# One decoder step on one core: row statistics, weight low halves, key pages and the first head pair are scheduled otherwise

## The chip, the cores and the metric

The kernel runs on one core of a Trainium2 chip. Its time is the device time of one launch in microseconds (us); the number that counts is the median over the runs. The core has five engines with a queue each, which work side by side and meet at semaphores: PE (TensorE, matrix products), DVE (VectorE), ACT (ScalarE), POOL (GpSimd) and SP, which here only issues DMAs. PE is the engine with most to do, so an idle microsecond on PE is, nearly always, a microsecond of the run. Each queue is served strictly in order: an instruction that waits holds up all that stands behind it on its engine, and this is what most of the text below is about.

## The reference, cut to what matters

One layer of a hybrid decoder trunk, for a prompt (1024 positions) and 8 samples with one new token each, 1024 columns wide, all in fp32.

```
h = rmsnorm(x);  z = h @ w_in                      # 2308 columns, in blocks of 512, 260, 512, 512, 512
A: softmax(q k^T / 8 + forget bias), causal        # prompt; samples read 32 pages of 128 old keys each
B: u * (W_s v + b), inside chunks of 128 positions
C: dilated window attention, three branches, joint softmax; samples read windows of old keys
M: softmax(q mem_k^T / 8) into 256 memory rows     # mem_k, mem_v = rmsnorm(mem) @ w_mem
x = x + concat(norm(A), norm(B), norm(C), norm(M)) @ w_out
x = x + down(silu(conv(gate)) * conv(value))       # ConvFFN, 2 x 2816 columns up
```

`rmsnorm` divides a row by the root of the mean of its squares; here the products run on the unnormalised rows and the factor of each row is applied to the result. For a sample, attention A needs the dot products of its query with 4096 paged keys, then the weighted sum of 4096 paged values.

## The kernel before, in words

Each fp32 operand is split into a high half that PE takes (`hhi`, `whi`) and a low half, the rest (`hlo`, `wlo`); a product is three matmuls, hi*hi, hi*lo, lo*hi (L847 to L849).

**Start.** 16 chunks of the transposed input (`x_load`, `x_hi` on ACT at L1138, `x_lo` on DVE at L1475) and 8 chunks of the first weight block (`w_load`, `split_hi` on ACT at L1127, `split_lo` on DVE at L1466) come in through SP's queue. Then the same rows are fetched a second time, in row layout (`stat_load`, L467, 11 fetches, three places to put them), and ACT squares and sums each (L1159). POOL turns all 11 sums at once into row factors (`inverse_rms`, L2091 and L2094), and only then does ACT begin to evacuate the first product (`rs_row`).

**Projection.** There are 47 units (`units`): 5 blocks of columns (b) times the 8 samples ("S") and 8 tiles of 128 prompt rows, and two units of memory rows (b = 5). A unit is 8 chunks times 3 matmuls into one of 4 banks. Behind a unit ACT evacuates or squares it, DVE sums the squares (L1510), POOL makes the factor, DVE applies it one turn later (`finish_norm`, L1522 and L1530); SP writes the result out two turns later. The loops of all engines over the units are written out by hand, and what else stands in a turn is in this order. `chunk_turns` says in which turn a chunk of the next weight block is split: chunks 0 to 3 in units 0 to 3 of the block before, chunks 4 and 5 in its last unit, chunks 6 and 7 in the "S" unit of the block itself. One granule of sample keys (4 pages, 512 KB, in a ring of 4) stands in each of 32 prompt turns of blocks 1 to 4, at the turn's end (`k_dot`, L1498 and L1501). Two pages of a granule are issued by SP, two by ACT, each after reading its page number (L353, L354). Block 2 has the small products of group B behind its units (`sgu`, L822), each with a DVE gate (L1557) before the next.

**Attention.** When the last unit is done and all outputs have landed, the first head pair is loaded (`qk_load(0)`, `toe_load`), transposed (`prep`, L894) and split. Then come 96 steps: 4 heads of A (steps 0 to 31), 4 of M (32 to 63), 4 of C (64 to 95), 8 query tiles each. In a step PE does scores, transposes and the product with the values, DVE the maximum (`score`), ACT the exponential. Steps 0 to 31 also carry the other 32 key granules, whose 4 pages SP issues three steps ahead; after the 32nd and 64th granule DVE takes the maxima, POOL reduces them over the partitions (`max_all`, L2114), DVE subtracts. 74 granules of sample values are added by PE (`v_sum`, L962) from step 4 on, by the table `v_step`; POOL issues all four pages of the first `V1` = 22, later POOL two and SP two.

**Rest.** Output projection and ConvFFN follow.

## Time and profile before

| what | us |
|---|---|
| median of 3 runs (range) | 1607.78 (1606.0 to 1610.24) |
| the profiled execution, its own time | 1605.6 |
| its span, first to last instruction | 1604.0 |
| start, until the sixth unit begins | 0 to 62.2 |
| projection, from there to the last unit's end | 62.2 to 317.8 |
| change-over to attention, until step 4 | 317.8 to 365.1 |
| steps 4 to 15, steps 16 to 31 | 54.1, 75.5 |
| steps 32 to 63 (heads of M) | 97.9 |
| steps 64 to 95 (heads of C) | 592.6 to 698.5 |
| output projection and ConvFFN | 698.5 to 1604.0 |

PE is busy for 91% of the span, DVE 60%, ACT 29%, POOL 10%. The last 905 us are nearly pure PE work and the change leaves them alone. A step is counted from the moment at which DVE writes its maximum. The profile's chain that ended last gives PE 66% of the span, SP's queue 9%, DVE 9%, waiting for nothing visible 7%.

### The profile page before, as it was taken

What the parts mean: (1) busy time and instruction counts of PE and PEld (TensorE: products, weight loads), DVE (VectorE), ACT (ScalarE), POOL (GpSimd) and SP (SyncE); (2) the same over time, 40 slices, a digit from 0 to 9 for tenths busy, and PEclk for the clock granted to TensorE, in tenths of its full rate; (3) what the DMA queues carried; (4) which work ended last, traced back from release to release, by engine and by line L of the source; (5) the groups of instructions that cost most, each with busy time, mean ns of one, the idle gap of its engine ahead of it and who ended that gap; (6) DMA issues with size and microseconds to landing.
All of it is one profiled execution on the core that took longest, in us unless ns stands there. A gap on an engine that the chain in (4) does not pass through costs nothing.

```text
span 1604.0 us, 25881 instructions
## 1 busy us (share of the span) xinstructions
PE 1464.0 (91%) x8727; PEld 1318.3 (82%) x8727; DVE 955.9 (60%) x1528; ACT 466.2 (29%) x723; POOL 163.3 (10%) x262
## 2 busy tenths in 40 slices
PE   6897989858889999778989999999999999999997
PEld 4686777646666667568989999999999999999997
DVE  5365467659987766482466655565646556555553
ACT  5322112233433456451232322222212222222210
POOL 0300022223322233200000000000000000000000
PEclk9998999956855579888999999999999999999999
DMA  7484335387667957322100220202102020120202
GB/s 262 154 252 141 115 115 174 115 242 207 203 200 231 299 176 219 110 85 109 59 27 12 68 67 14 73 8 80 54 27 67 14 81 27 53 67 14 79 1 116
DMA packets 123224, 177.11 MB, mean 110 GB/s; under 512 B 23005, under 2 KB 94198, under 8 KB 122674
## 3 DMA queue, kind: packets, MB, share of 16 engines
q1 hardware_dynamic: 105290, 140.17, 28.0%
q0 software_dynamic: 9728, 27.80, 5.8%
q10 hardware_dynamic: 8064, 7.34, 1.6%
q8 instruction: 78, 1.28, 0.3%
...
## 4 chain that ended last, share of the span: by engine, by line
PE 66%; SPq 9%; DVE 9%; issue 7%; DMA 4%; ACT 3%; POOL 1%; POOLq 0%; ACTq 0%; DVEq 0%; PEldq 0%
PE ps L1017 16%; PE ps L1018 16%; PE ps L1019 16%; SPq L353 4%; SPq L354 4%; PE ps L943 3%; PE ps L847 3%; PE ps L849 2%; PE ps L848 2%; PE ps L962 2%; PE ps L927 1%; DMA qb<-in_x_prompt 1%; PE ps L918 1%; DMA vring<-in_cache_a_v 1%; DVE ring L1498 1%
## 5 line engine op out<-in xcount | busy, mean ns | idle before, releaser
L1017 PE MATMUL ps<-hhi,uhi 128*128 128x344 f32 x1056 | 339.0, 321 | 11.9 <-DVE hlo L1964 4.9
L1018 PE MATMUL ps<-hlo,uhi 128*128 128x344 f32 x1056 | 337.8, 320 | 0.0
L1019 PE MATMUL ps<-hhi,ulo 128*128 128x344 f32 x1056 | 337.5, 320 | 0.0
L1017 PEld LDWEIGHTS ps<-hhi,uhi 128*128 128x128 f32 x1056 | 199.3, 189 | 13.7 <-issue 10.6
L1018 PEld LDWEIGHTS ps<-hlo,uhi 128*128 128x128 f32 x1056 | 199.3, 189 | 0.0
L1019 PEld LDWEIGHTS ps<-hhi,ulo 128*128 128x128 f32 x1056 | 199.3, 189 | 0.0
L1017 PE MATMUL ps<-ahi,dhi 128*128 128x344 f32 x528 | 170.4, 323 | 3.6 <-DVE dlo L2067 3.6
L1018 PE MATMUL ps<-alo,dhi 128*128 128x344 f32 x528 | 170.5, 323 | 0.0
L1019 PE MATMUL ps<-ahi,dlo 128*128 128x344 f32 x528 | 169.6, 321 | 0.0
L847 PE MATMUL ps<-whi,hhi 128*128 128x512 f32 (+1 forms) x376 | 147.3, 392 | 20.8 <-DVE wlo L1466 12.7
L943 PEld LDWEIGHTS ps<-vst,pts 128*128 128x128 f32 x704 | 110.6, 237 | 62.2 <-issue 41.8
L1996 DVE TENSOR_TENSOR uu<-ps,rstd_bc 128x1032 f32<-128x1032 f32 x44 | 54.3, 1233 | 178.8 <-PE ps L1019 178.8
L849 PE MATMUL ps<-whi,hlo 128*128 128x512 f32 (+1 forms) x376 | 143.9, 383 | 0.0
L848 PE MATMUL ps<-wlo,hhi 128*128 128x512 f32 (+1 forms) x376 | 143.7, 382 | 0.0
L943 PE MATMUL ps<-vst,pts 128*128 128x65 f32 x704 | 124.4, 329 | 14.0 <-DVE oN L1691 13.8
L354 POOL DMA_DIRECT2D vring<-in_cache_a_v x172 | 93.1, 541 | 184.3 <-issue 175.6
L2029 DVE TENSOR_TENSOR x<-ps,x 128x1032 f32<-128x1032 f32 x80 | 98.3, 1229 | 14.6 <-PE ps L1019 11.0
L847 PEld LDWEIGHTS ps<-whi,hhi 128*128 128x128 f32 x376 | 73.7, 196 | 39.6 <-DVE wlo L1466 16.0
L1017 PEld LDWEIGHTS ps<-ahi,dhi 128*128 128x128 f32 x528 | 100.1, 190 | 5.5 <-DVE dlo L2067 3.9
L1019 PEld LDWEIGHTS ps<-ahi,dlo 128*128 128x128 f32 x528 | 100.2, 190 | 0.0
L1018 PEld LDWEIGHTS ps<-alo,dhi 128*128 128x128 f32 x528 | 100.2, 190 | 0.0
L1370 ACT ACTIVATE convG<-uu,prm_a 128x1024 f32<-128x1024 f32 x22 | 27.4, 1247 | 202.0 <-DVE uu L1996 202.0
...
## 6 DMA issues: line engine op xcount, KB each, us to landing
...
```

What stands on the lines that cost most here:

```text
L353: page = sp.value_load(ptab[0:1, bass.ds(seq * PAGES + (group * 4 + j), 1)], min_val=0, max_val=NPOOL - 1)
L354: sp.dma_start(dst[:, slot, j, :], pool[bass.ds(page, 1)].rearrange("o p c -> p (o c)"))\
L847: pe.matmul(out, lh, whi[:, sl, 0:w], start=(kc == 0), stop=False)
L848: pe.matmul(out, lh, wlo[:, sl, 0:w], start=False, stop=False)
L849: i = pe.matmul(out, ll, whi[:, sl, 0:w], start=False, stop=(kc == KC - 1))
L943: i = pe.matmul(ps[:, 6, 0:HD + 1], pts[:, g % 2, j, :], vst[:, hp % 2, j, H % 2, :], start=(j == 0), stop=(j == nb - 1))
L962: m = pe.matmul(ps[32 * q:32 * q + NH, 7, 0:WG], e_, v, start=first, stop=final)
L1017: pe.matmul(out, lhs_hi(kc), rhs_hi(kc)[:, cs], start=(n == 0), stop=False)
L1018: pe.matmul(out, lhs_hi(kc), rhs_lo(kc)[:, cs], start=False, stop=False)
L1019: i = pe.matmul(out, lhs_lo(kc), rhs_hi(kc)[:, cs], start=False, stop=(n == nk - 1))
L1996: dve.tensor_tensor(c3(uu[:, :]), U3(k % 2), c3(rstd_bc[:, :]), ALU.mult).then_inc(S("f_free"), 1)
L2029: dve.tensor_tensor(c3(x2[:, d, :]), U3(d % 2), c3(x2[:, d, :]), ALU.add).then_inc(S("f_free"), 1)
```

## The change

1. **Statistics.** The second fetch of the 9 input row tiles is gone. ACT squares each staged chunk (`x_square`, 16 of 516 columns), POOL adds them (`x_add`, 14 adds), PE sums over the partitions with 9 products with a column of ones (`stats`), DVE copies the sums in two parts (`stat_copy`), POOL makes the factors in three parts, so the first four units wait for the first half alone. The two tiles of memory rows are still fetched, later (`mem_stats`). The constants' DMAs move from SP to ACT's queue. The sums over forget-gate pages move from behind the "S" unit to behind unit (0, 2).
2. **Low halves of weights.** After the first block `split_lo` runs on POOL, in POOL's turn. `chunk_turns` puts chunks 4 to 7 all in the last unit of the block before, and the loads run 4 chunks ahead of the splits.
3. **Key pages.** 48 granules, not 32, are spread over the turns from (0, 6) to (5, 1) (`K_AT`, by a table of room per block), the first of a turn at its start; steps 0 to 15 carry the other 16. The softmax preparation of the first half moves into block 4 (`early_softmax` at (4, 3), `subtract_a(0)` at (4, 6), `max_all` on POOL at (4, 5)), that of the second half from steps 32 and 35 to 16 and 19.
4. **Values.** `V0, V1, V2 = 8, 28, 44`: 8 granules by step 15 (all four pages on POOL), 20 in steps 16 to 31, 16 in steps 32 to 63, 30 after; from the 9th on SP issues two of four pages.
5. **First pair.** Its queries and keys are loaded at turn (2, 2) into places of their own, its transposes use banks 4 and 5 and stand right behind the last unit; SP loads rows, values and bias table ahead of the last output.

The core of the diff:

```diff
-                        turns[u if kc < 6 else UI[(b, "S")] if b < 5 else UI[(5, 0)]].append((b, kc))
+                    turns[UI[(b - 1, kc if kc < 4 else 7)]].append((b, kc))
...
+        NKP = 48
+        for u_, (b_, t_) in enumerate(units):
+            if u_ >= UI[(0, 6)]:
+                k_room[u_] = (2.9, 2.2, 4.1, 2.9, 3.6, 2.0)[b_]
...
-        V1, V2 = 22, 46
+        V0, V1, V2 = 8, 28, 44
...
-            for x in range(11):
-                stat_load(x)
...
+                if k == (2, 2):
...
+                    qk_load(0)
...
-            qk_load(0)
+            sp.wait_ge(S("z_done"), NU)
             sp.wait_ge(S("crow_dram"), 64)
             c_rows(0)
-            outputs(units[NU - 1])
-            for s4 in range(4):
-                uses = [k for k in prompt_no if prompt_no[k] % 4 == s4]
-                sp.wait_ge(S(f"zo_out{s4}"), 16 * sum(0 if k[0] == 2 else n_out[k[0]] for k in uses))
+            v_load(0)
             sp.wait_ge(S("toe_dram"), 80)
...
             toe_load(toeA[:, :], 0, "toeA_ld")
-            v_load(0)
             for n in range(NKP, NKP + 3):
                 k_load(n)
...
-                if g < 32:
+                if g < 16:
                     k_load(NKP + 3 + g)
...
+            def stats(half):
+
+                pe.wait_ge(S("x_acc"), 8 * half + 8)
...
+                for x, c0 in cols:
+                    m = pe.matmul(ps[:, 7, 288 + x:289 + x], sacx[:, c0:c0 + P], ones[:, 0:1], start=True, stop=True)
+                m.then_inc(S("st_pe"), 1)
...
                 if k == (0, "S"):
+                    pe.wait_ge(S("rtab"), 4)
+                    stats(0)
+                    page_transposes()
+                if k == (0, 2):
+                    page_sums()
+                    pe.wait_ge(S("st_cp"), 1)
+                    stats(1)
...
+            def x_square(i):
+
+                c = slice((i // 8) * 516, (i // 8) * 516 + 516)
+                if i % 8 == 0:
+                    act.activation(sacx[:, c], xslot(i)[:, 0:516], ACT.Square).then_inc(S("x_sq"), 1)
+                else:
...
+                    act.activation((sqt0 if i % 2 else sqt1)[:, :], xslot(i)[:, 0:516], ACT.Square).then_inc(S("x_sq"), 1)
...
+                act.wait_ge(S("rs_row"), 1 if u < 4 else 2 if b < 5 else 3)
...
-                for bb, kc in CT[u]:
-                    split_lo(bb * KC + kc)
...
+                if grans:
+                    granule(grans.pop(0))
...
+                if k == (4, 3):
+                    early_softmax()
+                if k == (4, 6):
+                    subtract_a(0)
...
+            for u, k in enumerate(units):
+                for bb, kc in CT[u]:
+                    split_lo(bb * KC + kc)
...
+                if k == (4, 5):
+                    max_all(1, 0, 0, 16)
...
-                if k == 25:
+                if k == 17:
                     max_all(2, 0, 16, 32)
```

Three places show how it moves instructions. First DVE in the middle of block 3, where a turn joins the granule (`ring`), the sum of squares (`ssn`), the application of the factor (`zn`, `zo`) and the split (`wlo`). Before:

```order
L1498 TENSOR_TENSOR ring<-ring,qb 128x1024 [waits ring_ld1,qb_ld]
L1501 TENSOR_REDUCE sA<-ring 128x16 [waits k_mul]
L1466 TENSOR_TENSOR wlo<-wst,whi 128x512 [waits w_hi]
L1510 TENSOR_REDUCE ssn<-sq 128x8 [waits rs_norm,act_z]
L1522 SCALAR_TENSOR_TENSOR zn<-ps,rsx,rsn 128x512 [waits zo_dve,rs_norm]
L1530 TENSOR_TENSOR zo<-zn,prm_b 128x256 [waits dve_z,zo_out1,ob_ready]
```

and now:

```order
L1546 TENSOR_TENSOR ring<-ring,qb 128x1024 [waits ring_ld0,qb_ld]
L1549 TENSOR_REDUCE sA<-ring 128x16 [waits k_mul]
L1570 SCALAR_TENSOR_TENSOR zn<-ps,rsx,rsn 128x512 [waits zo_dve,rs_norm]
L1578 TENSOR_TENSOR zo<-zn,prm_b 128x256 [waits dve_z,zo_out2,ob_ready]
L1558 TENSOR_REDUCE ssn<-sq 128x8 [waits rs_norm,act_z]
```

The split with its wait for ACT (`w_hi`) has left DVE, and the wait for the unit itself (`act_z`) now stands behind the granule and the factor.

Second POOL at units (4, 5) to (4, 7), where `ISA small<-small` is the reduction over the partitions and a bare `ISA` exchanges the library that POOL's program is taken from. Before, the first reduction stands behind the last of the first 16 value pages (page number read, DMA), after the projection:

```order
L353 TENSOR_LOAD ptab
L353 ISA x2
L354 ISA
L354 DMA vring<-in_cache_a_v 128x256
L2114 ISA
L2114 ISA small<-small 128x16 [waits pm]
```

and now between normalisations of the projection:

```order
L2147 TENSOR_TENSOR rsn<-rsn,nhalf 128x4 [waits pool_chain]
L2150 ISA
L2150 ISA small<-small 128x16 [waits pm]
L2144 ISA
L2144 TENSOR_SCALAR rsn<-ssn 128x4 [waits zo_dve,ss_dve]
L2147 TENSOR_TENSOR rsn<-rsn,nhalf 128x4 [waits pool_chain]
L2165 TENSOR_TENSOR wlo<-wst,whi 128x512 [waits w_hi] x4
```

Two exchanges and the reduction stand ahead of the factor of unit (4, 6) and of the last four splits, which unit (5, 0) needs.

Third SP behind the last unit. Before:

```order
L572 DMA qst<-scr_q 128x8x128 [waits zo_out2,zo_out1,zo_out3,zo_out0,z_done]
L573 DMA kst<-o_ka 128x8x128
L591 DMA klc<-scr_c 2x1024 [waits crow_dram]
L516 DMA o_mk<-zo 128x256 [waits act_z,zo_dve]
L516 DMA o_mv<-zo 128x256
L587 DMA toeA<-scr_t 128x1024 [waits toe_dram,zo_dve,zo_out3,ob_out0,zo_out2,ob_out1,zo_out1,zo_out0]
```

and now:

```order
L582 DMA klc<-scr_c 2x1024 [waits crow_dram,z_done]
L573 DMA vst<-o_va 128x8x64 x2
L578 DMA toeA<-scr_t 128x1024 [waits zo_out0,toe_dram]
L356 TENSOR_LOAD ptab [waits k_used]
L356 ISA x2
L357 ISA
L357 DMA ring<-in_cache_a_k 128x256
```

The last output and the wait for it no longer stand between the last unit and the bias table and the key pages.

## Rows read from the trace of the kernel before

**Rows 1.** Stretches: start:end, us, busy us (x count) by engine, granted clock, DMA share, GB/s

```profile
62.20:69.96 7.76, 7.75 (x24) 6.17 (x25) 5.41 (x12) 0.03 (x1) 4.93 (x5) 0.70 0.57 174
62.20:317.80 255.60, 231.73 (x1077) 190.13 (x1077) 154.98 (x249) 54.44 (x102) 41.67 (x51) 0.94 0.51 155
87.08:118.56 31.48, 28.24 (x217) 27.59 (x217) 22.95 (x34) 7.66 (x16) 1.83 (x2) 0.95 0.90 270
118.56:131.44 12.88, 8.23 (x25) 5.73 (x25) 8.18 (x13) 6.06 (x10) 0.00 (x0) 0.74 0.95 313
143.13:163.10 19.97, 15.88 (x66) 12.97 (x65) 7.33 (x12) 3.59 (x7) 0.00 (x0) 0.83 0.20 60
189.50:222.90 33.40, 26.96 (x114) 21.74 (x114) 13.63 (x29) 4.99 (x8) 6.36 (x6) 0.90 0.23 68
264.10:297.40 33.30, 33.30 (x145) 27.01 (x144) 23.46 (x36) 10.15 (x23) 6.02 (x10) 1.00 0.55 170
317.80:365.10 47.30, 22.93 (x104) 18.98 (x105) 25.66 (x51) 15.65 (x22) 12.88 (x23) 0.63 0.79 225
365.10:419.20 54.10, 47.14 (x293) 35.27 (x292) 49.77 (x97) 21.99 (x39) 19.37 (x36) 0.72 0.69 204
419.20:494.70 75.50, 64.87 (x391) 49.42 (x390) 64.57 (x126) 26.18 (x45) 20.44 (x38) 0.70 0.65 191
494.70:592.60 97.90, 93.16 (x499) 60.70 (x500) 66.35 (x160) 43.52 (x124) 28.22 (x53) 0.59 0.82 252
592.60:633.20 40.60, 39.71 (x361) 29.82 (x359) 30.23 (x87) 26.16 (x50) 16.55 (x30) 1.00 0.84 250
698.50:1604.00 905.50, 869.61 (x5442) 862.59 (x5441) 499.35 (x596) 210.89 (x215) 3.84 (x6) 0.98 0.16 51
```

**Rows 2.** Chain of waits in the start: start us, us, what

```profile
29.24 4.90 DMA qb<-in_x_prompt
...
46.07 5.23 DMA qb<-in_mem
```

**Rows 3.** Instructions in order of time at the first evacuation: start us, us

```profile
52.56 0.23 POOL L2091 TENSOR_SCALAR rsx<-ssx 128x11 f32<-128x11 f32 x1 [41.33 <-ACT biasA L1159]
...
62.21 0.77 PE L847 MATMUL ps<-whi,hhi 128*128 128x512 f32 x1 [6.76 <-issue]
```

**Rows 4.** Who waited in 62 to 318: total us, times, longest us

```profile
PE ps L847 <- DVE wlo L1466: 11.6, 6, 2.7
...
PE ps L822 <- DVE ob L1557: 6.4, 2, 4.1
...
DVE wlo L1466 <- ACT whi L1127: 26.4, 9, 5.5
```

**Rows 5.** Groups of DVE in 0 to 340: busy us, mean ns | idle before

```profile
L1501 DVE TENSOR_REDUCE sA<-ring 128x16 f32<-128x1024 f32 x32 | 39.0, 1220 | 1.1
L1498 DVE TENSOR_TENSOR ring<-ring,qb 128x1024 f32<-128x1024 f32 x32 | 39.0, 1218 | 0.2 <-DVE zs L1530 0.2
L1466 DVE TENSOR_TENSOR wlo<-wst,whi 128x512 fp32r<-128x512 f32 x40 | 26.7, 685 | 22.0 <-ACT whi L1127 21.8
```

**Rows 6.** Groups of POOL in the whole span

```profile
L2094 POOL TENSOR_TENSOR rsn<-rsn,nhalf 128x8 f32<-128x8 f32 x16 | 26.2, 1638 | 1.3
...
L2083 POOL TENSOR_SCALAR_AFFINE_SELECT wsT<-wsT 128x512 f32<-128x512 f32 x1 | 0.7, 659 | 0.4 <-issue 0.4
```

**Rows 7.** POOL in order of time at its first reduction over partitions

```profile
345.58 0.39 POOL L2114 PARTITION_ALL_REDUCE small<-small  x1 [5.98 <-issue]
```

**Rows 8.** DVE and SP in order of time in the change-over

```profile
328.91 0.33 SPq L587 DMA_DIRECT2D toeA<-scr_t  x1
328.99 0.09 DVE L1628 MEMSET vst<- 128x32 f32 x1 [7.37 <-DMA o_mv<-zo]
...
354.76 39.42 SPq L354 DMA_DIRECT2D ring<-in_cache_a_k  x36
```

**Rows 9.** PE's groups of sample values, 64 granules, in 0 to 720

```profile
L962 PE MATMUL ps<-vring,sA 128*4 128x256 f32 x512 | 52.2, 494 | 4.4 <-DMA vring<-in_cache_a_v 3.5 <-ACT mkd L1256 0.8
```

624 lines of the change are left out of this document (335 added, 289 removed).

## The prediction

> **What bounds the kernel now.** I first cut the span into stages and read busy time and granted clock of each [rows 1]. Behind 698.5 PE is busy for 869.6 of 905.5 us at clock 0.98, and the change has nothing there. What there is to win lies before. In the projection a unit at full clock takes 33.30/6 = 5.55 us (PE 33.30 busy in 33.30 us, clock 1.00) and a unit of block 1 about half, yet 255.6 us pass. In the change-over PE is busy for 22.9 of 47.3 us. In steps 4 to 31 it is DVE (49.8 of 54.1, 64.6 of 75.5 us) and SP that fill the time. In steps 32 to 63 PE is busy for 93.2 of 97.9 us, at clock 0.59, the lower of the two levels most of the time (1.2 against 2.4 GHz). The second view is the chain of waits in the start [rows 2]: four rounds of the second fetch, the first at 29.24, the last landing at 51.3. Then the instructions in order of time [rows 3]: POOL's factors come at 52.6 and the sixth unit starts at 62.21, after 6.76 us without work. Third, who waits for whom [rows 4].
>
> **Start.** What goes is the second fetch. In its place ACT has 16 squares of 516 columns. I take 0.7 us each, by DVE's 0.685 for 512 columns [rows 5], and as much for each high half, so ACT spends some 2.1 us on a chunk of the first half and 1.4 on one of the second: about 23 us to the end of the first half, 37 to the end of the second, 41 with DVE's scan behind it, against 52.6 + 2.2 before. PE: "S" unit until 24, sums and transposes until 28.5, three units of 5.55 until 45.2, page sums (four products of 512 columns in plain fp32, some 5 us by estimate) and the second sums until 51.8, then unit (0, 3). It ends at 57.4, its banks are free by then, and the sixth unit starts at 57.4, not 62.2: **-4.8 us**. It then runs at full clock behind a PE that did not stand still: **-2.2** (before, it took 7.76 us at clock 0.70 [rows 1]). Between 0 and -10 is possible.
>
> **Low halves.** Block 1 takes 31.5 us where 9 units of 2.86 make 25.7; the "S" unit of block 2 takes 12.9 us at clock 0.74 where 5.55 do [rows 1]: 13.0 us lost in these two, about 2 more at block 4. PE names the cause, `wlo` of DVE: 11.6 us in 6 waits; DVE in turn stood before these splits for 26.4 us, waiting for ACT [rows 4], with all its other work behind. The new table puts the last four chunks a whole unit earlier and out of DVE's queue. The price of a subtraction of 128x512 on POOL is in no row. Bounds: 0.66 us (a select with one such input) and 1.64 us (the power of 8 columns, much slower per column) [rows 6]; DVE needs 0.685 [rows 5]. I take 1.2, nearer the first end because it does two inputs. POOL starts a last turn about 4 us after its unit began, ends four splits at 8.8, and PE wants the last chunk at 5.55 + 7/8 of 5.55 = 10.4; at 1.64 it would be 10.6. So the 15 us go: **-15** (0 to -15). The Trainium skill, "GPSIMD Engine Reference", section 3.1, gives 4497 ns for a two-input fp32 addition of 2048 elements, so as an estimate 1.1 us here; no trace of before shows it, and the sum would be the same.
>
> What remains of the waits of the projection is block 2's chain of small products and gates: 143.1 to 163.1 is two units and two gates' products (12.9) in 20.0 us, 189.5 to 222.9 four units (24) in 33.4 [rows 1, 4]: 16.5 us, which I keep. One new wait comes: POOL's reduction in turn (4, 5). Before, it stood 5.98 us without visible cause before its first reduction [rows 7]; the order shows a library exchange there. Now there are two, 12.4 us with the reduction. Behind them wait the factor of (4, 6) and the last four splits, and for these unit (5, 0): the first is done some 19 us after unit (4, 6) began, and PE wants it at 13.9. With the four splits that is 7 us where 2.9 were lost before: **+4** (0 to +10). DVE gets 16 more granules at 1.218 + 1.220 = 2.44 us, 39 us, plus 4 us of softmax, and loses 40 splits, 25 us [rows 5]: 173 of some 242 us, which fits on the whole, hardly in block 4. PE runs up to three units ahead, so I cost it at nothing; if that cover fails, up to +8. The last unit ends at 317.8 - 4.8 - 2.2 - 15 + 4 = **299.8**.
>
> **Change-over.** SP's bias table went out at 328.9, 11.1 us behind the last unit, since it waited for the last output to land; DVE waited 7.37 us for the same [rows 8]. Now three short issues (2.6 us) stand before it. Behind it stand the same 12 key pages and the same small loads, the output's two issues (0.8) added. Step 4 comes when the first granule issued behind these has landed, so it is SP's queue that sets it: 11.1 - 2.6 + some 2 us of waits for landed outputs that go from there make **-10.3**. The early transposes and the earlier first steps are hidden behind it; without SP they would give some more. Bounds 0 and -15.
>
> **Steps 4 to 15.** SP issues 36 pages in 39.42 us [rows 8], 1.095 each, 4.38 a step, against 54.1/12 = 4.51: SP is the bound, DVE close behind. The number of granules in these steps is the same. Two pairs of value pages stand ahead of the last key loads: 4 x 1.1 = **+4.4** (0 to +8.8, where all four pairs count).
>
> **Steps 16 to 31.** DVE loses 16 x 2.44 = 39 of 64.6 us, SP 64 pages and gains 40, 2.75 us a step; POOL has 40 pages, 2.5 a step; in steps 64 to 77 both had 19 granules in 13 steps, 2.9 pages a step, and kept up. PE is next. Steps 64 to 77 are the same code with the same tiles and even more values a step: 40.6/13 = 3.12 us a step, at clock 1.00 [rows 1]. 16 x 3.12 = 50. One new wait: the second reduction needs another exchange, and in POOL's order it stands behind the load of granule 16, which waits for the sum of granule 12 in step 19, the step in which DVE wants the result: 2.3 + 6 + 0.4 us, less 1.5 that DVE is behind, less what the pipeline takes up: +5. 75.5 - 55 = **-20.5**. The other end is PE's own busy time at clock 0.70, 64.9 us, plus the 5: -5.5.
>
> **Steps 32 to 95.** 16 value granules in place of 24, at 52.2/64 = 0.82 us each [rows 9], in a stage that PE bounds except where DVE has the window keys: **-5** of 6.6. Behind that two more: **+1.6**.
>
> **Sum**, against the profiled execution's own 1605.6: -4.8 - 2.2 - 15 + 4 - 10.3 + 4.4 - 20.5 - 5 + 1.6 = -47.8, so 1557.8. The median of the runs shown is 2.2 above that execution, so **1560**.
>
> **Rivals.** A, the clock stays down. In steps 4 to 31 it is 0.72 and 0.70, and steps 32 to 63 had 0.59 although PE hardly stood still [rows 1]. Then steps 16 to 31 are PE-bound at 4.05 us: 1560 + 15 = 1575. Against it: steps 64 to 77, directly behind the stage at 0.59, had 1.00. B, the projection gives little, since DVE's granules at the head of each turn, ACT's page issues and the exchange on POOL take back what the splits free: the last unit at 315, 1575. For it: in block 4 DVE has 1.4 granules a unit, 3.4 us, and with normalisation and the memory rows by estimate some 5.6 of 5.55 us; against it, 100 us idle on DVE in the projection. C, more than forecast: the gates no longer wait, as finishing a norm no longer stands between a unit and its gate, and the exchange is hidden: 1560 - 12 - 6 = 1542. D, slower: POOL's subtractions shut DVE out. Forty at c us are added to DVE's 173; with 57.4 at the start and 25 us of waits, the last unit ends at 255.4 + 40c. The other terms give 29.8 us, so the loss begins where this passes 347.6, at c = 2.3 us; at 2.6 it is 359.4, and the run 1560 + 60 = 1620. For it: POOL's per-element price is unknown, and a granule's multiplication and a split both read two tiles. Against it: before, POOL's powers ran beside DVE's granules and these show 1218 ns on average, no spread worth naming. The Trainium skill, "GPSIMD Engine Reference", section 1, says that GpSimd and VectorE share their SBUF interfaces and contend when a DVE instruction has two SBUF inputs. No row of before shows the two together; by that rule alone and an estimate of 1.1 us a split, DVE would have up to 44 us more and the projection would end some 10 us later, which is B's time, not D's.
>
> **Chances.** Forecast 0.50, A 0.20, B 0.15, C 0.08, D 0.07. A and B together would be 1590. The range 1540 to 1588 takes in A, B and the bounds of the terms; the forecast's own is 1548 to 1570. A measurement of this kernel tells 0.3% (5 us) from no change: faster 0.92, same 0.02, slower 0.06.
>
> **What would show it.** No second fetch before 50 us, POOL's adds at 1.1 to 1.3 us, the sixth unit at 57; no wait of PE for `wlo` but in unit (5, 0), the last unit's end near 300; DVE's multiplications still at 1218 ns; step 4 some 37 us after the last unit; steps 16 to 31 in 55 us at a clock near 1.00, with a hole at 19. Wrong it would be if the splits take over 2 us or stretch DVE's work, if the last unit ends behind 312, or if steps 16 to 31 keep 0.7 of the clock.

## The result and the profile after

The changed kernel is slower: 1632.61 us median of 4 runs (1619.29 to 1638.29) beside 1609.01 (1606.0 to 1610.66) of the kernel before, ratio 1.014, 95% interval 1.007 to 1.020. Run again beside experiments 9 to 11, it had 1623.27 us (6 runs, 1619.4 to 1628.81), ratio 1.008 (1.005 to 1.011). So the loss is 13 to 22 us by the two ratios, where 48 us of gain were forecast; the profiled execution shown here (1638.29 us, span 1635.5) is the slowest of the ten. One execution of the kernel before, at 1822.98 us and a granted clock of 0.72 (the others 0.91 to 0.93), is in no ratio of this document. In the new source the lines have moved: products 856 to 858, GpSimd's subtraction 2165, its addition of squares 2160, page products 1546.

By stages, in the columns of [rows 1] (the five busy times are those of PE, its weight loads, DVE, ACT and POOL): the start, block 1 with the "S" unit in front of it, the "S" unit of block 2, block 4 up to turn (4, 5), the rest of the projection, the change-over, steps 4 to 15, 16 to 31, 32 to 63, 64 to 94, and what follows.

```profile
0.00:61.96 61.96, 45.88 (x166) 33.10 (x167) 40.54 (x51) 29.28 (x51) 33.53 (x33) 0.92 0.43 141
84.63:120.05 35.42, 29.45 (x216) 28.75 (x217) 22.94 (x29) 5.13 (x10) 15.53 (x14) 0.90 0.78 244
120.05:137.95 17.90, 7.76 (x24) 5.46 (x25) 12.45 (x14) 5.61 (x11) 6.60 (x4) 0.71 0.77 256
261.20:294.75 33.55, 33.54 (x144) 27.03 (x145) 24.77 (x30) 7.36 (x15) 17.68 (x16) 1.00 0.67 204
294.75:355.30 60.55, 37.29 (x121) 27.77 (x119) 37.03 (x55) 9.71 (x22) 17.78 (x19) 0.72 0.34 104
355.30:395.80 40.50, 23.11 (x105) 18.46 (x105) 21.01 (x39) 13.75 (x21) 13.92 (x23) 0.62 0.80 230
395.80:453.90 58.10, 47.88 (x292) 37.02 (x290) 50.16 (x98) 22.10 (x39) 11.84 (x22) 0.71 0.59 173
453.90:519.55 65.65, 58.90 (x427) 44.42 (x429) 31.31 (x103) 27.42 (x47) 20.31 (x38) 0.79 0.64 192
519.55:610.60 91.05, 78.33 (x447) 53.81 (x440) 63.19 (x148) 42.96 (x122) 18.73 (x36) 0.70 0.65 198
610.60:729.75 119.15, 99.70 (x829) 76.87 (x821) 70.87 (x217) 58.87 (x115) 29.15 (x44) 0.90 0.52 153
729.75:1635.50 905.75, 868.35 (x5419) 860.57 (x5419) 495.94 (x584) 209.40 (x211) 3.84 (x6) 0.98 0.15 51
```

The profiled span is 31.5 us longer where 47.8 less were forecast. Most of the miss is the projection: its last unit ends at 355.3, not 299.8, 37.5 us later than before. Behind it stand -6.7 in the change-over (forecast -10.3), +4.0 in steps 4 to 15 (+4.4), -9.8 in steps 16 to 31 (-20.5), -6.8 in 32 to 63 (-5) and +8.7 in 64 to 94 (+1.6), in the sum -10.6 for -29.8. For the last of these the stretch before ends at 703.0; the table of times before stops at 698.5, which is the maximum of step 94. What follows is 4.7 us longer (905.75 for 901.0) with the same work; in the sixteen other profiles it takes 898 to 910 us, so this is no effect of the change, and the stages in front of it are the better measure.

Up to 294.75 the projection is only 8.4 us behind; two stretches around a change of block carry most of that (35.42 and 17.90 us, before 31.48 and 12.88). The last 60.55 us then hold five units that took 31.5 us before; PE is busy for 37.3 of them, DVE for 37.0, POOL for 17.8, ACT for 9.7: a chain of waits, not work.

The waits of PE in 62 to 355 us (us, times, longest), against [rows 4], where `wlo` stood at 11.6:

```profile
PE ps L856 <- POOL wlo L2165: 31.0, 6, 14.3
PE ps L856 <- DVE zn L1570: 8.4, 2, 4.6
```

POOL's groups in the whole span, against [rows 5, 6]: the price of a subtraction of 512 columns that the prediction had to bound, with 78.3 us in which POOL stood before these subtractions and waited for ACT's high halves, and the price of an addition.

```profile
L2165 POOL TENSOR_TENSOR wlo<-wst,whi 128x512 fp32r<-128x512 f32 x32 | 47.0, 1483 | 78.3 <-ACT whi L1145 78.3
...
L2160 POOL TENSOR_TENSOR sacx<-sacx,sqt 128x516 f32<-128x516 f32 x14 | 20.7, 1481 | 1.7
```

In the change-over SP's bias table now goes out 1.65 us behind the last unit, not 11.1 [rows 8]:

```profile
356.95 0.53 SPq L578 DMA_DIRECT2D toeA<-scr_t  x1
```

Four mechanisms can be read from the order of time. First, GpSimd beside DVE in the start. DVE, then POOL (start us, us, instruction, idle before):

```profile
20.17 1.78 DVE L1511 TENSOR_TENSOR wlo<-wst,whi 128x512 fp32r<-128x512 f32 x1
21.87 1.78 DVE L1520 SCALAR_TENSOR_TENSOR hlo<-x,prm_a,hhi 128x516 fp32r<-128x516 f32 x1
...
26.97 0.68 DVE L1511 TENSOR_TENSOR wlo<-wst,whi 128x512 fp32r<-128x512 f32 x1
27.57 0.74 DVE L1520 SCALAR_TENSOR_TENSOR hlo<-x,prm_a,hhi 128x516 fp32r<-128x516 f32 x1
```
```profile
15.54 10.95 POOL L2160 TENSOR_TENSOR sacx<-sacx,sqt 128x516 f32<-128x516 f32 x7
32.41 0.62 POOL L2144 TENSOR_SCALAR rsx<-ssx 128x4 f32<-128x4 f32 x1 [5.93 <-DVE ssx L1507]
```

The seven additions run until 26.49; beside them a DVE operation of two inputs takes 1.78 us, right behind them 0.68 and 0.74. ACT waits as well, 3.40 us until 16.85, for the first addition, which stands behind GpSimd's table loads; but DVE has no gap between 15.0 and 28.9, so it is DVE's pace that sets the "S" unit's end here.

Second, the change to block 2. ACT, then POOL:

```profile
123.95 0.47 ACT L1230 ACTIVATE zo<-ps,rsx 128x256 f32<-128x256 f32 x1 [9.24 <-DMA o_va<-zo]
...
129.80 2.18 ACT L1145 ACTIVATE whi<-wst 128x512 fp32r<-128x512 f32 x4
```
```profile
130.50 6.60 POOL L2165 TENSOR_TENSOR wlo<-wst,whi 128x512 fp32r<-128x512 f32 x4 [17.41 <-ACT whi L1145]
```

The four high halves stand in ACT's queue behind evacuations, and three of these wait 9.24, 2.24 and 2.29 us until earlier outputs of block 1 have landed and their place is free. SP issued those outputs behind weight loads and pages, the first at 114.89, and they landed 5.7 us after their issue in the median (3.6 before). GpSimd cannot begin before.

Third, a ring of queues in block 4. SP, then POOL, then ACT:

```profile
289.37 0.42 SPq L501 DMA_DIRECT2D scr_q<-zo  x1
296.42 0.34 SPq L460 DMA_DIRECT2D wst<-in_w_mem  x1
296.81 0.91 SPq L472 DMA_DIRECT2D xst<-in_memT  x2
...
304.41 9.30 SPq L357 DMA_DIRECT2D ring<-in_cache_a_k  x4
...
314.71 1.00 SPq L472 DMA_DIRECT2D xst<-in_memT  x2
```
```profile
293.85 0.19 POOL L2144 TENSOR_SCALAR rsn<-ssn 128x4 f32<-128x4 f32 x1 [8.52 <-DVE ssn L1558]
294.13 1.01 POOL L2147 TENSOR_TENSOR rsn<-rsn,nhalf 128x4 f32<-128x4 f32 x1
295.11 1.29 POOL L2165 TENSOR_TENSOR wlo<-wst,whi 128x512 fp32r<-128x512 f32 x1
```
```profile
299.43 0.51 ACT L1156 ACTIVATE hhi<-xst,prm_a 128x256 fp32r<-128x256 f32 x1 [7.21 <-DMA xst<-in_memT]
...
318.52 0.91 ACT L1156 ACTIVATE hhi<-xst,prm_a 128x256 fp32r<-128x256 f32 x2 [11.64 <-DMA xst<-in_memT]
```

SP's weight load at 296.42 goes out 0.02 us behind the end of POOL's subtraction (295.11 + 1.29). Its slot is the one which that subtraction frees: the new list loads four ahead, so the load issued in a turn needs the low half of the same turn. The fetch of the memory rows stands behind it, ACT waits 7.21 us for that fetch, DVE waits for ACT, its sum of squares stands behind, and POOL's next factor waits 8.62 us for that sum. So the fetches of turns (4, 2) and (4, 3) lie 11.1 us apart (285.74 and 296.81) where PE needs 5.55. The subtraction at 295.11 is the last before turn (4, 7); behind it the queues hold each other up over the pages. At 304.41 four page loads, two products' worth, take 9.30 us in SP's queue, as the second pair waits for a product that DVE reaches at 309.07, behind the softmax preparation that was moved here; the next fetch goes at 314.71, and ACT waits 11.64 us for it. POOL's factors come 11.2, 10.2 and 8.4 us apart.

Fourth, GpSimd around its first reduction over partitions, against [rows 7], and then at step 19:

```profile
331.45 0.39 POOL L2150 PARTITION_ALL_REDUCE small<-small  x1 [5.58 <-issue]
339.45 0.19 POOL L2144 TENSOR_SCALAR rsn<-ssn 128x4 f32<-128x4 f32 x1 [7.62 <-issue]
339.73 1.06 POOL L2147 TENSOR_TENSOR rsn<-rsn,nhalf 128x4 f32<-128x4 f32 x1
340.77 6.13 POOL L2165 TENSOR_TENSOR wlo<-wst,whi 128x512 fp32r<-128x512 f32 x4
```
```profile
473.88 0.39 POOL L2150 PARTITION_ALL_REDUCE small<-small  x1 [7.37 <-issue]
```

It stands idle without a releaser on both sides of the reduction, and the four subtractions that unit (5, 0) needs come behind: PE waits 14.31 us in one piece, and that unit takes 25.6 us (before 8.5). The exchange recurs at 473.88, so steps 19 to 20 take 13.7 us.

### The profile page after: what moved, and what is told of

Read it like the earlier page. It is cut to its first block, busy times and chain, and to the rows that moved or that the text cites. A ratio compares the mean times of both kernels' runs of the same rounds, so it can differ in the third digit from the quotient of the medians.

```text
span 1635.5 us, 25981 instructions
## 1 busy us (share of the span) xinstructions
PE 1463.0 (89%) x8745; PEld 1320.4 (81%) x8745; DVE 959.1 (59%) x1490; ACT 461.9 (28%) x720; POOL 238.2 (15%) x293
## 4 chain that ended last, share of the span: by engine, by line
PE 65%; DVE 7%; issue 6%; SPq 4%; DMA 3%; POOL 2%; ACT 2%; POOLq 0%; ACTq 0%; DVEq 0%; PEldq 0%
PE ps L1035 16%; PE ps L1036 16%; PE ps L1037 16%; PE ps L957 4%; SPq L356 2%; PE ps L856 2%; PE ps L858 2%; PE ps L857 2%; PE ps L976 2%; SPq L357 1%; DMA vring<-in_cache_a_v 1%; PE ps L941 1%; PE ps L908 1%; PE ps L932 1%; DVE ring L1546 1%
## 5 line engine op out<-in xcount | busy, mean ns | idle before, releaser
L1035 PE MATMUL ps<-hhi,uhi 128*128 128x344 f32 x1056 | 339.5, 322 | 12.4 <-DVE ulo L1996 5.0
L1035 PEld LDWEIGHTS ps<-hhi,uhi 128*128 128x128 f32 x1056 | 199.7, 189 | 14.3 <-issue 11.2
L856 PE MATMUL ps<-whi,hhi 128*128 128x512 f32 (+1 forms) x376 | 152.8, 406 | 44.7 <-POOL wlo L2165 31.0
L957 PEld LDWEIGHTS ps<-vst,pts 128*128 128x128 f32 x704 | 107.8, 232 | 62.8 <-issue 33.8
L857 PE MATMUL ps<-wlo,hhi 128*128 128x512 f32 (+1 forms) x376 | 148.2, 394 | 0.0
L858 PE MATMUL ps<-whi,hlo 128*128 128x512 f32 (+1 forms) x376 | 148.0, 394 | 0.0
L957 PE MATMUL ps<-vst,pts 128*128 128x65 f32 x704 | 121.1, 323 | 20.4 <-DVE oN L1820 20.2
L1546 DVE TENSOR_TENSOR ring<-ring,qb 128x1024 f32<-128x1024 f32 x64 | 83.0, 1297 | 38.4 <-DMA ring<-in_cache_a_k 38.4
L357 POOL DMA_DIRECT2D vring<-in_cache_a_v x144 | 77.9, 541 | 185.9 <-issue 163.2
```

The costliest lines, as they stand in the source:

```text
L357: sp.dma_start(dst[:, slot, j, :], pool[bass.ds(page, 1)].rearrange("o p c -> p (o c)"))\
L856: pe.matmul(out, lh, whi[:, sl, 0:w], start=(kc == 0), stop=False)
L857: pe.matmul(out, lh, wlo[:, sl, 0:w], start=False, stop=False)
L858: i = pe.matmul(out, ll, whi[:, sl, 0:w], start=False, stop=(kc == KC - 1))
L957: i = pe.matmul(ps[:, 6, 0:HD + 1], pts[:, g % 2, j, :], vst[:, hp % 2, j, H % 2, :], start=(j == 0), stop=(j == nb - 1))
L1035: pe.matmul(out, lhs_hi(kc), rhs_hi(kc)[:, cs], start=(n == 0), stop=False)
```

## The experiments

T1 is the ring through SP; T2 the two engines holding each other up; T3 the exchanges of GpSimd's code around the reduction; T4 the turns with two page products, whose loads stand in SP's and ACT's queues. The table has microseconds of each profiled execution: start of units (0, 0), (2, 0), (4, 5) and (5, 0), end of the last unit, steps 4, 32 and 95, then the median and the ratio to the kernel before with its interval. Each ratio is to runs of the kernel before that were made beside it (their medians lie between 1606.8 and 1609.7 us). Where the starts are the same code, (0, 0) still differs by up to 1.2 us, so single differences of that size say nothing.

| kernel | (0,0) | (2,0) | (4,5) | (5,0) | end | step 4 | 32 | 95 | median | ratio |
|---|---|---|---|---|---|---|---|---|---|---|
| before | 32.7 | 131.4 | 286.3 | 303.5 | 317.8 | 365.1 | 494.7 | 703.0 | 1609 | 1 |
| changed, 2nd time | 33.9 | 136.5 | 291.9 | 319.6 | 351.6 | 390.3 | 511.8 | 720.5 | 1623.3 | 1.008 (1.005-1.011) |
| 1 loads 3 ahead | 33.7 | 131.2 | 288.3 | 307.9 | 339.2 | 379.3 | 498.7 | 711.4 | 1613.4 | 1.005 (1.002-1.008) |
| 2 reduction behind | 33.6 | 135.8 | 291.3 | 319.3 | 343.1 | 384.4 | 492.8 | 700.6 | 1607.5 | 1.000 (0.997-1.002) |
| 3 low halves DVE | 33.4 | 132.8 | 302.1 | 327.7 | 349.7 | 393.8 | 515.4 | 723.0 | 1627.3 | 1.014 (1.008-1.020) |
| 4 six row slots | 33.8 | 135.8 | 291.7 | 308.9 | 337.1 | 377.5 | 496.8 | 706.2 | 1613.9 | 1.003 (1.000-1.007) |
| 5 = 2, 32 products | 33.6 | 134.5 | 285.6 | 304.0 | 321.4 | 360.4 | 489.7 | 699.3 | 1602.9 | 0.997 (0.995-0.999) |
| 6 = 1 + 2 + 4 | 33.6 | 132.8 | 291.1 | 308.3 | 325.9 | 366.8 | 479.9 | 687.9 | 1593.4 | 0.989 (0.984-0.995) |
| 7 = 6, 40 products | 32.4 | 133.4 | 283.6 | 300.8 | 312.2 | 352.7 | 467.5 | 672.0 | 1573.4 | 0.979 (0.975-0.984) |
| 8 = 7, last 4 on DVE | 33.6 | 139.7 | 290.9 | 308.1 | 319.5 | 359.2 | 473.5 | 677.4 | 1582.3 | 0.985 (0.980-0.989) |
| 9 = 7, no additions | 25.4 | 121.3 | 271.7 | 288.9 | 300.4 | 342.2 | 456.3 | 658.8 | 1560.3 | 0.969 (0.966-0.972) |
| 10 = 7, all on DVE | 33.6 | 143.1 | 291.7 | 308.9 | 320.3 | 360.7 | 475.2 | 678.9 | 1584.0 | 0.984 (0.981-0.987) |
| 11 = 7, 32 products | 33.4 | 129.7 | 279.4 | 296.6 | 308.0 | 348.8 | 479.3 | 688.3 | 1590.2 | 0.988 (0.984-0.991) |
| 12 = 7, adds on DVE | 27.9 | 124.0 | 272.7 | 289.9 | 301.3 | 341.9 | 456.7 | 661.2 | 1564.5 | 0.973 (0.969-0.978) |
| 13 = 12, 4 ahead | 28.4 | 130.6 | 279.3 | 296.6 | 307.9 | 348.7 | 463.4 | 667.9 | 1568.6 | 0.975 (0.970-0.979) |
| 14 adds on DVE only | 27.8 | 126.3 | 281.8 | 309.9 | 341.7 | 381.1 | 505.6 | 713.6 | 1616.6 | 1.006 (1.004-1.008) |

**1, weight loads three ahead.**

```diff
- CT_load = {u: [b * KC + kc + 4 for b, kc in CT[u] if b * KC + kc + 4 < 6 * KC] for u in range(NU)}
+ CT_load = {u: [b * KC + kc + 3 for b, kc in CT[u] if b * KC + kc + 3 < 6 * KC] for u in range(NU)}
- for q in range(KC, KC + 4):
+ for q in range(KC, KC + 3):
```

> One edit to the changed kernel: SP issues the weight loads three chunks ahead instead of four, so that the load issued in a turn waits for the subtraction of the turn before and no longer for that of its own turn. Theory T1 (SP's queue is tied to POOL: each load waits for POOL's subtraction of the same turn, and the memory rows, the pages and the outputs stand behind it): the turns of block 4 fall from 10.5 us on ACT, DVE and POOL to about 8.5, the last unit ends near 335 instead of 355.3, and the time falls by some 15 to 20 us. Rival T2 (POOL's subtractions are slow because they and the DVE's operations hold each other up, 1.48 us in the mean instead of 1.29): nothing changes but a few us, last unit 350 to 358. Rival T3 (library exchanges of GpSimd around the all-reduce at turn (4,5)): the same as T2, and unit (5,0) still takes over 20 us.

Units (4, 6) and (4, 7) start 5.5 us apart as before, the last unit ends 12.4 us earlier than in the changed kernel's second profile and step 95 comes 9.1 us earlier. The ratio falls from 1.008 to 1.005; the two intervals overlap, so the worth of this edit (and of the fourth) is read from the profiles. The ring is real, the gain half of what T1 said. The "S" unit of block 2 shows the same tie: it takes 17.1 to 21.1 us in the eight kernels that load four ahead and 9.8 to 13.5 in the six that load three ahead with all subtractions on GpSimd. Unit (5, 0) keeps 24.9 us (T3 and T4). ACT in that kernel shows T4's part: the high halves of the last four chunks stand behind four page loads.

```profile
308.08 5.08 ACTq L357 DMA_DIRECT2D ring<-in_cache_a_k  x4
313.25 1.67 ACT L1145 ACTIVATE whi<-wst 128x512 fp32r<-128x512 f32 x3 [6.09 <-issue]
317.86 0.63 ACT L1145 ACTIVATE whi<-wst 128x512 fp32r<-128x512 f32 x1 [2.93 <-DMA wst<-in_w_mem]
```

**2, the reduction behind the projection.**

```diff
-                if k == (4, 5):
-                    max_all(1, 0, 0, 16)
...
             pool.memset(q1c[HD:HD + 2, :, :].bitcast(f32), 1.0).then_inc(S("q_ones"), 1)
+            pool.wait_ge(S("q_ones"), 1)
+            max_all(1, 0, 0, 16)
@ DVE
-                if k == (4, 6):
-                    subtract_a(0)
...
+                if g == 1:
+                    subtract_a(0)
```

> One edit to the changed kernel: the first all-reduce of the sample softmax is issued behind the projection phase, as before the change, and what it feeds (the first subtraction of the maxima on DVE) at step 1 of attention. So GpSimd has no library exchange between its arithmetic in the projection. T3 (exchanges): the 5.58 and 7.62 us of idle time around the all-reduce at 331 us go, unit (5,0) takes 8 to 12 us instead of 25.6, the last unit ends at 340 to 345; if the hole of 13.7 us at step 20 is also an exchange, it stays (the second all-reduce is still there) but is no longer; time 10 to 20 us less. T1 (SP tied to POOL): the turns (4,2) to (4,6) still take 10.5 us each, and the last unit still ends over 335. T2 (contention) forecasts the same as T1 here, with subtractions at 1.48 us in the mean.

Unit (5, 0) takes 16.7 us instead of 25.6 (24.8 in the second profile), and steps 19 to 20 take 5.4 instead of 13.7 (14.1): one edit takes two holes of 8 to 9 us, since with the code exchanged once for good the second reduction finds it in place. T3 is shown, and by the time of the run it is the largest single cause: step 95 comes 19.9 us earlier and all of the loss against before goes (ratio 1.000). Steps 16 to 31 fall to 50.7 us, at a granted clock of 0.94 where it was 0.79 and 0.84. Unit (5, 0) stays above the 8 to 12 us expected, which leaves room for T4. The first reduction still has its idle time, now where nobody waits as long for it, and the second has none:

```profile
354.07 0.39 POOL L2150 PARTITION_ALL_REDUCE small<-small  x1 [6.14 <-issue]
...
453.94 0.34 POOL L2150 PARTITION_ALL_REDUCE small<-small  x1
```

**3, low halves on DVE again, at the head of each turn.**

```diff
@ GpSimd, each turn
-                for bb, kc in CT[u]:
-                    split_lo(bb * KC + kc)
@ DVE, each turn
+                for bb, kc in CT[u]:
+                    split_lo(bb * KC + kc)
```

> One edit to the changed kernel: the low halves of the weights are computed on DVE again, at the head of each turn, in the turns of the new table; GpSimd keeps only the sums of squares, the inverse norms and the all-reduces. T2 (GpSimd's subtractions and DVE's operations hold each other up): the DVE multiplication of the key pages falls from 1297 ns in the mean to 1220, a subtraction costs 0.70 us on DVE, the turns of block 4 fall from 10.5 to about 8 us and the last unit ends at 320 to 325; time near 1600. T3 adds to it: nothing on GpSimd is late behind the all-reduce but the factor of zn. Rival T4 (two page products in some turns and the page loads in SP's and ACT's queues are the cause, whoever subtracts): DVE carries 0.7 us more a turn and the last unit still ends at 345 or later, time within 10 us of 1632.

T2 is right on the size: the page products fall to 1218 ns, so GpSimd's subtractions cost them 48 x 0.106 = 5 us in all. As the cause it fails: the last unit still ends at 349.7. That is a sum of two parts, though: from unit (2, 0) to (4, 5) this kernel loses 13.8 us on the second profile, and from there to the end it gains 12.1, so the experiment alone does not clear the subtractions; the tenth does. DVE's groups in 0 to 355 us, first the changed kernel's, then this one's:

```profile
L1546 DVE TENSOR_TENSOR ring<-ring,qb 128x1024 f32<-128x1024 f32 x48 | 63.5, 1324 | 23.1 <-DMA ring<-in_cache_a_k 23.1
```
```profile
L1546 DVE TENSOR_TENSOR ring<-ring,qb 128x1024 f32<-128x1024 f32 x48 | 58.5, 1218 | 8.3 <-DMA ring<-in_cache_a_k 8.3
```

**4, six slots for the memory rows.**

```diff
-                    sp.wait_ge(S("x_split"), i - 1)
+                    sp.wait_ge(S("x_split"), i - 5)
...
-                if b == 4 and tt != "S" and tt >= 2 and tt < 6:
-                    for i in (2 * (tt - 2), 2 * (tt - 2) + 1):
+                if k in ((4, "S"), (4, 4)):
+                    for i in (range(6) if tt == "S" else (6, 7)):
```

> One edit to the changed kernel: the chunks of the memory rows get six slots instead of two, and are fetched at turns (4,S) (six) and (4,4) (two) instead of two a turn behind the subtraction of the chunks before. The chain in each turn of block 4 was: fetch lands, ACT's high half, DVE's low half, DVE's page product, GpSimd's inverse norm, GpSimd's subtraction, and then SP's next weight load with the next fetch behind it. T1 (this round through SP is what sets 10.5 us a turn): the ACT wait for the fetched rows (27.7 us in 5 waits) goes, the turns (4,2) to (4,6) fall to about 8 us, last unit at 335 to 340, 15 to 20 us less. T2 (contention): 5 us less at most. T3: no change, and (5,0) still over 20 us since the exchanges are there.

ACT's 27.7 us of waits for these rows are gone, the last unit ends 14.6 us earlier than in the second profile, step 95 comes 14.3 us earlier. Cutting the ring at either place gives nearly the same at the last unit.

**5 to 8.** In the fifth and seventh the table that hands page products to turns is replaced (`NKP = 32`, one a turn of blocks 1 to 4; `NKP = 40`, one a turn from (0, 6) on), with attention's own steps shifted to match and the value pages in the table of before. The sixth joins experiments 1, 2 and 4. The eighth:

```diff
@ GpSimd, each turn
                 for bb, kc in CT[u]:
-                    split_lo(bb * KC + kc)
+                    if kc < 4:
+                        if kc == 0:
+                            pool.wait_ge(S("w_split"), bb * KC)
+                        split_lo(bb * KC + kc)
@ DVE, end of each turn: the same for kc >= 4
```

> The second experiment (all-reduce behind the projection) with the page tables of before: 32 page products in the projection, one a turn, the first in block 1, none in a turn of its own beside another; 32 in attention; the value pages in the table of before, all four by GpSimd up to group 21. T4 (turns with two products have SP and ACT issue four page loads each that wait for DVE, 5 to 9 us, and the high halves of the last four chunks of block 5 and the memory rows stand behind): unit (5,0) falls from 16.7 us in the second experiment to 10 us or less, the turns of block 4 to 6 to 8 us, the last unit ends at 322 or earlier against 343; attention's steps 16 to 32 take again some 75 us instead of 51; in the sum 1600 to 1610, so that the wider table is worth nothing. T1 (SP tied to POOL alone): unit (5,0) stays over 14 us and the last unit ends after 335; then the time is 1620 or more. The 3 us wait for value pages at step 67 goes in both, since fewer groups fall in the last steps.

> Three of the earlier experiments in one: weight loads three ahead, the memory rows in six slots, the all-reduce behind the projection. If their causes are separate (T1 in the queues, T3 on GpSimd), the gains add up in part: the turns of block 4 at 6 to 8 us, unit (5,0) 12 to 15 us (T4's late high halves stay), the last unit ends near 322, the hole at step 20 at 5 us; time near 1590, below before. If T1's two edits remove the same wait (both showed the same gain), it is 1595. Rival: a limit that they share (DVE's own work in block 4, 8.5 us in a turn with two products): no better than 1605.

> The sixth experiment with a page table of 40 products in the projection, just one a turn from turn (0,6) on, and 24 in attention; the value pages in the step table of before. T4: no engine has a turn with two products, the high halves of the last four chunks of block 5 are not behind four page loads, unit (5,0) takes about 10 us and the last unit ends near 315, attention has 8 products more to do (8 x 2.45 us on DVE, part of it beside PE): steps up to 32 take some 10 us more than in the sixth; time 1585 to 1590. Against T4: unit (5,0) as in the sixth, time 5 to 10 us above the sixth.

> The seventh experiment with the low halves of the last four chunks of each block on DVE, the first four on GpSimd. These four are computed in a row between the end of one block and the first unit of the next, where PE waits for them: 4 x 1.5 us on GpSimd, 4 x 0.70 on DVE. T5 (the size of the subtraction on GpSimd is on the path at each change of block): units (1,S), (2,S), (3,S), (4,S) and (5,0) each end 2 to 3.3 us earlier (the products of half-width blocks less), 8 to 12 us in the sum; time 1575 to 1580. Rival: DVE reaches them later than GpSimd, since they stand behind its page product and its zn of the turn: no change or slower by up to 5 us.

The fifth: the last unit ends at 321.4 against 343.1 in the second; the ring is still there, so this is T4 or the sixteen products fewer. The sixth: the gains add up in part (the last unit ends at 325.9; at step 95 32.6 us are gained where the three by themselves had 43). The seventh: better than any theory said, 1573 us. Unit (5, 0) takes 5.7 us (11.9 in the sixth), and step 4 comes 14.1 us earlier. The count alone does not explain that: from 40 to 32 products, still one a turn, the last unit gains only 4.2 us (eleventh), where from 48 to 40 it gains 13.7. So the double turns are what costs, and T4 is shown.

From step 4 on the seventh also has the value table of before, and the record shows what that is worth. Steps 64 to 76 take 40.6 to 41.7 us in the kernel before and in the eight that have its value table (5 and 7 to 13), and 45.0 to 51.4 in the eight profiles with the new one, which leaves 30 granules for the steps from 64 on where the other leaves 28. (The page table changes with it, but its products are done by step 32.) In the changed kernel's first profile PE waits 4.3 us for value pages there and the granted clock is 0.90, in the second 1.1 us at 0.98; in the seventh it is 0.2 us at 1.00.

The eighth refutes T5: PE now waits longer, for DVE, which comes to these chunks behind its other work of the turn (eighth, then seventh):

```profile
PE ps L846 <- DVE wlo L1501: 18.3, 2, 9.2
```
```profile
PE ps L846 <- POOL wlo L2155: 13.4, 5, 5.1
```

**9 to 11 and the changed kernel again.** The ninth leaves out the additions of the squares, so its row statistics hold one chunk of eight. The tenth is the seventh with all low halves on DVE, at the end of each turn; the eleventh is the seventh with the page and value tables of before. The ninth's edit:

```diff
-                if i % 8 > 1:
-                    pool.wait_ge(S("x_acc"), i)
-                pool.tensor_tensor(sacx[:, c], sacx[:, c], (sqt0 if i % 2 else sqt1)[:, :], ALU.add).then_inc(S("x_acc"), 1)
+                pool.sem_inc(S("x_acc"), 1)
```

> The changed kernel itself, once more, beside the others of this call: its first four runs lay between 1619 and 1638 us. Every theory forecasts 1.0137 times the kernel before within the interval; a median under 1620 would mean that the gains of the single edits were measured against a bad run.

> The seventh experiment without GpSimd's 14 additions of the squares (ACT computes the squares as before; the row statistics then hold only the first chunk's, so their values are wrong, but no operation downstream changes its time). T2 for the first 62 us (the additions and DVE's low halves hold each other up, 1.78 us an operation instead of 0.68 to 0.75, and ACT's squares wait for the additions): unit (0,0) starts at 28 to 30 instead of 32.4 to 33.6 and everything behind it as much earlier, time 3 to 5 us less than the seventh. Rival: the start is set by the transfers of the first chunks and tables (DMA), and the additions are beside them: unit (0,0) starts within 1 us of the seventh's, the time is the same.

> The seventh experiment with all low halves of the weights behind the start on DVE again, at the end of each turn: the value of GpSimd's subtractions once the queues are mended. The prediction gave them 15 us. If that holds: DVE's 40 subtractions of 0.70 us stand in turns that already have 4 us of other work under 5.6 us of PE, block 3 and 4 turn to DVE's pace, 1583 to 1588. Rival (the third experiment, where moving them back to DVE cost nothing, 1627 against 1633): within 4 us of 1573.

> The seventh experiment with the page and value tables of before (32 products in the projection): the value of more pages in the projection once the queues are mended. Eight products of 2.45 us on DVE move back to attention's steps 24 to 32, which DVE bounds: 1573 + 10 to 15, that is 1583 to 1588, the last unit ends 2 to 4 us earlier than in the seventh. Rival: the projection gives back as much as attention takes: within 4 us of 1573. The fifth experiment (1603, same tables, queues not mended) says what the queues are worth alone: 15 to 20 us.

The changed kernel's second median lies above the 1620 named in the expectation; its interval is the narrower one, and gains of single edits are read against it. The ninth moved unit (0, 0) by 7 us and the time by 13, three times what was expected. The tenth: once the queues are mended, GpSimd's subtractions are worth about 0.5% (8.1 us at the last unit, of which 1.2 lie at (0, 0) already; the intervals just overlap), the direction of the prediction's term and half its size. So the subtractions on GpSimd are a gain and T2 is refuted for the projection. The eleventh: eight products fewer in the projection end it 4.2 us earlier, and steps 16 to 31 take 74.9 us instead of 59.5; 40, one a turn, beats both 32 and the table with 48.

**12 to 14, the additions on DVE.**

```diff
@ DVE, start
             for kc in range(KC):
                 x_lo(kc)
                 split_lo(kc)
+                x_add(kc)
...
             for i in range(8, 16):
                 x_lo(i)
+                x_add(i)
```

GpSimd's loops over `x_add` go.

> The seventh experiment with the 14 additions of the squares on DVE instead of GpSimd, each right behind the low halves of its chunk; nothing is left out. The ninth (no additions) had unit (0,0) at 25.4 us against 32.4, and DVE's low halves at 0.68 to 0.75 us against 1.76 to 1.80. T2 for the start (what costs is GpSimd and DVE at once, not the additions): seven additions of 0.7 us on DVE ahead of unit (0,0) add about 5 us to the ninth's start, (0,0) at 29 to 31, unit (1,0) some 4 us earlier than the seventh's 94.7, time 1566 to 1570. Rival (the amount of work counts, wherever it is): (0,0) at 32 or later, time 1573 or more.

> The twelfth with weight loads four ahead again, as in the changed kernel: is the load that waits for GpSimd's subtraction of its own turn a cost by itself, or only where memory rows, double pages and the all-reduce stand with it? T1: block 4 stays at 5.6 us a turn since the memory rows have their slots, but blocks 2 and 3 end later as in the changed kernel (unit (2,0) at 137.9 there against 131.2 with three ahead): 4 to 8 us slower than the twelfth. Rival: nothing to wait for once the other two are mended, within 2 us of the twelfth.

> One edit to the changed kernel: the 14 additions of the squares on DVE. T2 for the start: unit (0,0) at 29 to 31 instead of 33.6. If what follows keeps the lead, the time falls by 3 to 5 us; if the queues of block 4 take it back (T1, as they did with DVE's own turns), by less than 2.

T2 is shown for the start: the same 14 additions, on DVE, let unit (0, 0) start at 27.9. Up to the end of the "S" unit's last low half DVE has eight splits from 18.9 to 28.9 us in the changed kernel, and the same eight and four additions from 18.3 to 25.9 in the twelfth. DVE's groups there, of the seventh and of the twelfth (busy us, mean ns):

```profile
L1510 DVE SCALAR_TENSOR_TENSOR hlo<-x,prm_a,hhi 128x516 fp32r<-128x516 f32 x16 | 18.3, 1163 | 9.3 <-ACT hhi L1146 9.2
```
```profile
L1510 DVE SCALAR_TENSOR_TENSOR hlo<-x,prm_a,hhi 128x516 fp32r<-128x516 f32 x16 | 11.8, 744 | 5.9 <-ACT hhi L1146 5.9
L1522 DVE TENSOR_TENSOR sacx<-sacx,sqt 128x516 f32<-128x516 f32 x14 | 9.5, 681 | 0.0
```

One addition on DVE costs 0.68 us; on GpSimd it costs 1.48 us there and 1.0 us on each DVE operation beside it. In the changed kernel (14) the same lead of 6 us is still 6.9 us at step 95, more than the 3 to 5 expected and against the rival's under 2; by the two ratios it is 3.9 us, with intervals that overlap. Four ahead (13) costs 6.7 us at the last unit and at step 95; the ratios, 0.9745 and 0.9733, do not tell them apart, so T1's edit by itself is shown in the profile only.

## Why the prediction was wrong

**Start, forecast -4.8 and -2.2.** The failed step is the additions of the squares beside DVE at no cost. The prediction had unit (0, 0) at 28.5, it came at 33.6; from there on its sum holds, in part by luck: the three units took 18.4 us and not 16.7, page sums and second sums 4.3 and not 6.6, and the sixth unit came 28.4 us behind against 28.9. (ACT's end of the second half, 37 us, should be 34 by the prediction's own prices; nothing hangs on it.) The -2.2 came as forecast (7.75 us from the sixth to the seventh unit before, 5.56 now). With the additions on DVE unit (0, 0) starts at 27.9 and the sixth at 54.8. The page that rival D cites, the Trainium skill, "GPSIMD Engine Reference", section 1 (shared interfaces, contention with DVE instructions of two SBUF inputs), was right here: 1.78 us for 0.68. The prediction applied it to the subtractions and not to the additions, which run back to back.

**Low halves, forecast -15.** The price was nearly right: 1.29 us alone, 1.53 in a row of four, 1.48 in the mean (forecast 1.2). The failed step is "POOL starts a last turn about 4 us after its unit began". In the change to block 2 the last turn's unit began at 116.7 and POOL its four subtractions at 130.5, 13.8 us later, with the unit (2, S) waiting since 120.05. [rows 4] had the reason: DVE stood before these splits for 26.4 us because ACT's high halves were late, and the new place takes DVE's queue away and not ACT's; POOL now stands for 78.3. From (1, S) to (2, 0), where 13.0 of the 15 us were to be gained, before took 44.4 us and this kernel 53.3; no kernel of this record takes less than 45.1 there. The 2 us at block 4 came ((4, S) 5.8 us for 7.4). The sum had a slip as well: it lets PE want the last chunk at 10.4 us by a last unit of 5.55, but a unit of block 1 takes 2.9 to 3.0, so by its own terms PE wants it at 7.7, a microsecond before the 8.8.

What made the loss larger than before is the order of SP's queue, which had not been followed: the prediction named what stood behind the moved subtraction on GpSimd, and not that the moved weight load waits for it on SP, with memory rows, pages and outputs behind. Experiments 1, 4 and 13 show that wait. Why outputs land later in block 1 than before (5.7 us for 3.6 in the median) was not tested; that more pages move beside them is one possible reason.

**The exchange, forecast +4 and +5.** Both idle times were foreseen, with their sizes (12.4 us for the pair, 13.6 measured). Their place was not: experiment 2 takes 8.9 us out of unit (5, 0) and 8.3 out of steps 19 to 20, and in a projection already late nothing was ahead to take them up. The first, +4, was within its bounds; the sum of the terms around it was not. The Trainium skill, "GPSIMD Engine Reference", section 2.1, gives about 6 us for the first call of a freshly loaded kernel; the traces are near it before the first reduction (5.5 to 6.4 us in all runs), show 7.4 to 9.5 before the second where arithmetic lay between, and 6.7 to 7.6 on the way back to arithmetic.

**The pages, forecast at nothing, up to +8.** DVE's busy time in block 4 is not what counted (24.77 of 33.55 us up to turn (4, 5)): the page loads of a double turn take 4 to 9 us of SP's and ACT's queues, and the high halves wait behind. The prediction counted DVE's microseconds and not the queue slots of the loads. From 48 products with double turns to 40 without, the last unit gained 13.7 us.

**Behind the projection.** The change-over (-6.7 for -10.3), steps 4 to 15 and 32 to 63 hold within 4 us. Steps 16 to 31 gave 9.8 of 20.5: the hole was 9 us and not 5, and the clock stood at 0.79. Without the hole the stage takes 50.7 us at a clock of 0.94 (experiment 2) and 54.9 at 0.88 (experiment 6), beside the forecast's 50 at 1.00. The six profiles with the hole have 0.79 to 0.87. So rival A is half right: the clock stayed between the two levels, and at least part of its loss goes with the hole. Steps 64 to 94 lost 8.7, for 1.6: the prediction took its two granules more at PE's price alone, and the value table costs 4 to 11 us in steps 64 to 76, as the runs with either table show.

**The time.** B said that pages, issues and exchange would take back the projection's gain, which is the right list at a quarter of its size (15 us on the last unit for 55). D, the slower case, was priced by a subtraction over 2.3 us, which is false; at 1.1 us its formula gives 299.4, the forecast itself, and not the 10 us later that its last sentence has. No case had the waits in a ring. C looked for a gain behind the change to block 2, and the kernels without double turns have one: from unit (2, 0) to (4, 5) they take 148.5 to 151.2 us (experiments 5 and 7 to 13), before 154.9. Its gates still wait, though (4.8 us in the twelfth, 6.4 before). The twelfth ends its projection at 301.3 (forecast 299.8), has step 4 40.6 us behind (37), steps 16 to 31 in 59.5 (55), and 1564.5 us (1560). That this is near the forecast is luck in good part. It is another kernel: additions on DVE, loads three ahead, six row slots, the reduction behind, 40 products one a turn, the value table of before; its steps 16 to 31 carry eight products that the forecast's do not, and the gain in its projection lies in blocks 2 to 4 (9.1 us from (2, 0) to the end) and not in the change to block 2 (2.2 us longer than before). Its stages from the sixth unit on:

```profile
54.80:301.27 246.47, 226.37 (x1078) 186.08 (x1076) 164.95 (x231) 58.73 (x114) 104.57 (x91) 0.97 0.60 183
301.27:341.90 40.63, 22.63 (x104) 18.58 (x105) 21.80 (x42) 13.75 (x21) 14.17 (x24) 0.65 0.82 233
341.90:397.20 55.30, 46.27 (x295) 35.20 (x294) 49.95 (x98) 22.06 (x39) 19.34 (x36) 0.75 0.69 202
397.20:456.70 59.50, 52.80 (x376) 40.84 (x379) 49.65 (x120) 27.05 (x46) 19.73 (x37) 0.81 0.76 220
```

It beats both kernels: 2.7% faster than before (2.2 to 3.1%), 3.5% faster than the changed one by the two ratios.
